# Splitting a weight tile into high and low parts in two halves instead of in one piece

## What is computed

```python
z = h @ w_in                                   # 2048 x (pool, 9 x dilated q/k/v, GLA q,k,v,r,a, 3 gates)
y = branches(z)                                # pooling, dilated attention, gated linear attention (GLA)
y = (sum of gated branches @ w_br_*) @ w_mix_out
x = x + rmsnorm(y);  x = x + rmsnorm(cross_attn(rmsnorm(x), mem_kv, w_xq, w_xo))
x = x + rmsnorm(conv_ffn(rmsnorm(x), w_up, conv_w, conv_b, w_down))
```

## Time and profile before

| | us |
|---|---|
| median of 3 runs | 2735.86 (2730.3 to 2737.19) |
| the profiled execution | 2728.69 |
| its span, first to last instruction | 2727.0 |
| mean granted clock of PE, share of full | 0.985 |
| PE busy | 2611.6 (96%) |
| DVE busy | 1549.4 (57%) |
| ACT busy | 1225.0 (45%) |
| DMA, moved | 530.80 MB, 195 GB/s |

### The profile page before, as it was taken

How to read it: one execution, slowest core, us unless ns; L and a number is a source line. 1 busy time by engine, 2 the same in 40 slices (tenths; PEclk the granted TensorE clock), 3 DMA queues, 4 the chain that set the end, 5 groups by cost and what they waited for, 6 DMA issues and landing times. The chain is left out here.

```text
span 2727.0 us, 52522 instructions
## 1 busy us (share of the span) xinstructions
PE 2611.6 (96%) x20839; PEld 2495.9 (92%) x20839; DVE 1549.4 (57%) x1940; ACT 1225.0 (45%) x1534; POOL 193.3 (7%) x303
## 2 busy tenths in 40 slices
PE   6799999999999999999999998999899999999997
PEld 5778879899999999999999988898799999999997
DVE  4455554544555555654564547454766665666666
ACT  5344444432443443443343544334555555444553
POOL 0011121100011111100000000320000000000000
PEclk9899999999999999999999999999899999999998
DMA  5686786766888888885666755865366656666563
GB/s 148 180 275 194 228 278 195 240 183 166 234 231 229 220 237 236 220 224 162 178 172 180 233 138 153 278 208 167 97 185 182 168 169 196 182 182 185 162 178 115
DMA packets 856553, 530.80 MB, mean 195 GB/s; under 512 B 13169, under 2 KB 834345, under 8 KB 855647
## 3 DMA queue, kind: packets, MB, share of 16 engines
q1 hardware_dynamic: 822583, 440.07, 58.8%
q0 software_dynamic: 25728, 83.34, 9.0%
q10 hardware_dynamic: 8128, 5.76, 0.7%
HBM read 499.79 MB, written 33.29 MB: 195 GB/s over the span
## 5 line engine op out<-in xcount | busy, mean ns | idle before, releaser
L518 DVE TENSOR_TENSOR weights_lo<-weights_raw,weights_hi 128x2048 fp32r<-128x2048 f32 x407 | 932.3, 2291 | 769.9 <-ACT weights_hi L511 769.1
L542 PE MATMUL bank<-h_hi,weights_hi 128*128 128x264 f32 x4624 | 1333.3, 288 | 35.8 <-DVE weights_lo L518 15.7
L543 PE MATMUL bank<-h_lo,weights_hi 128*128 128x264 f32 x4624 | 1314.6, 284 | 0.0
L544 PE MATMUL bank<-h_hi,weights_lo 128*128 128x264 f32 x4624 | 1313.1, 284 | 0.0
L542 PEld LDWEIGHTS bank<-h_hi,weights_hi 128*128 128x128 f32 x4624 | 875.5, 189 | 57.3 <-issue 26.2
L543 PEld LDWEIGHTS bank<-h_lo,weights_hi 128*128 128x128 f32 x4624 | 876.2, 189 | 2.0 <-issue 1.9
L511 ACT ACTIVATE weights_hi<-weights_raw 128x2048 fp32r<-128x2048 f32 x407 | 776.9, 1910 | 214.8 <-PE bank L544 205.0
L544 PEld LDWEIGHTS bank<-h_hi,weights_lo 128*128 128x128 f32 x4624 | 871.3, 188 | 0.0
L542 PE MATMUL bank<-y_hi,weights_hi 128*128 128x264 f32 x1232 | 351.9, 286 | 7.3 <-DVE y_lo L2413 3.8
L544 PE MATMUL bank<-y_hi,weights_lo 128*128 128x264 f32 x1232 | 350.6, 285 | 0.0
L543 PE MATMUL bank<-y_lo,weights_hi 128*128 128x264 f32 x1232 | 349.0, 283 | 0.0
(11 more groups left out here) (374 smaller groups left out, 2169.3 us busy)
## 6 DMA issues: line engine op xcount, KB each, us to landing
weights_raw<-in_w_in SPq DMA_DIRECT2D x177, 1024.0 KB, 6.6
weights_raw<-in_w_up SPq DMA_DIRECT2D x88, 1024.0 KB, 5.9
weights_raw<-in_w_down SPq DMA_DIRECT2D x64, 704.0 KB, 4.7
gla_state_sample<-in_state_gla POOLq DMA_DIRECT2D x32, 512.0 KB, 6.2
out_gla_s<-gla_state_sample POOLq DMA_DIRECT2D x32, 512.0 KB, 6.9
weights_raw<-in_w_br_gla SPq DMA_DIRECT2D x16, 1024.0 KB, 5.9
weights_raw<-in_w_mix_out SPq DMA_DIRECT2D x16, 1024.0 KB, 5.9
weights_raw<-in_w_xkv SPq DMA_DIRECT2D x16, 1024.0 KB, 6.0
```

Source lines behind the costliest of these rows:

```text
L518: nc.vector.tensor_tensor(w_lo[:, r, :], raw[:, r, :], w_hi[:, r, :].bitcast(F32), ALU.subtract).then_inc(lo_ready, 1)
L542: nc.tensor.matmul(out, wh, xh, start=first and n == 0, stop=False)
L543: nc.tensor.matmul(out, wh, xl, start=False, stop=False)
L544: mm = nc.tensor.matmul(out, wl, xh, start=False, stop=last and n == len(blocks) - 1)
```

## The change

Each tile is split in two halves of eight contraction blocks (1024 columns of the 2048). ACT issues two copies and counts `hi_ready` up after each; DVE waits for each half of the high part by itself, subtracts it, and counts `lo_ready` up after each. A product waits for the first half ahead of its first block and for the second half ahead of the first block that lies in it. A load waits for both halves. All counts on the two semaphores are doubled. Where two products share a tile (`fresh=False` in the second of them), only one that starts with the second half waits for it.

```diff
-        credits = [(lo_ready, RING)] + [(s, 1) for s in evac]
+        credits = [(lo_ready, 2 * RING)] + [(s, 1) for s in evac]
...
+        HALVES = [slice(0, SLOT // 2), slice(SLOT // 2, SLOT)]
...
             act.wait_ge(slot_loaded[r], (p.third(j, i) + 2) * 16)
-            nc.scalar.activation(w_hi[:, r, :], raw[:, r, :], ACT.Copy).then_inc(hi_ready, 1)
+            for half in HALVES:
+                nc.scalar.activation(w_hi[:, r, half], raw[:, r, half], ACT.Copy).then_inc(hi_ready, 1)
...
-            dve.wait_ge(hi_ready, p.c(j, i) + RING + 1)
             dve.wait_ge(projected, p.c(j, i) + 1)
-            nc.vector.tensor_tensor(w_lo[:, r, :], raw[:, r, :], w_hi[:, r, :].bitcast(F32),
-                                    ALU.subtract).then_inc(lo_ready, 1)
+            for n, half in enumerate(HALVES):
+                dve.wait_ge(hi_ready, p.c(j, i) * 2 + (2 * RING + 1 + n))
+                nc.vector.tensor_tensor(w_lo[:, r, half], raw[:, r, half], w_hi[:, r, half].bitcast(F32),
+                                        ALU.subtract).then_inc(lo_ready, 1)
...
-            sp.wait_ge(lo_ready, p.c(j, i) + 1)
+            sp.wait_ge(lo_ready, p.c(j, i) * 2 + 2)
...
             if fresh:
-                pe.wait_ge(lo_ready, p.c(j, i) + RING + 1)
+                pe.wait_ge(lo_ready, p.c(j, i) * 2 + (2 * RING + 1))
+            second = [n for n, b in enumerate(blocks) if b[0] >= SLOT // 2 and (fresh or b[0] == SLOT // 2)][:1]
...
                 wh, wl = w_hi[:, r, off:off + P], w_lo[:, r, off:off + P]
+                if n in second:
+                    pe.wait_ge(lo_ready, p.c(j, i) * 2 + (2 * RING + 2))
```

More of the change, by code:

```diff
@@ L959, in first_hi @@
                 act.wait_ge(slot_loaded[c], 16)
-                nc.scalar.activation(w_hi[:, c, :], raw[:, c, :], ACT.Copy).then_inc(hi_ready, 1)
+                for half in HALVES:
+                    nc.scalar.activation(w_hi[:, c, half], raw[:, c, half], ACT.Copy).then_inc(hi_ready, 1)
             first_hi(0)
@@ L2040, in first_lo @@
             def first_lo(c):
-                dve.wait_ge(hi_ready, c + 1)
-                nc.vector.tensor_tensor(w_lo[:, c, :], raw[:, c, :], w_hi[:, c, :].bitcast(F32),
-                                        ALU.subtract).then_inc(lo_ready, 1)
+                for n, half in enumerate(HALVES):
+                    dve.wait_ge(hi_ready, 2 * c + 1 + n)
+                    nc.vector.tensor_tensor(w_lo[:, c, half], raw[:, c, half], w_hi[:, c, half].bitcast(F32),
+                                            ALU.subtract).then_inc(lo_ready, 1)
             for t in range(KB):
```

## The result

| | before | after |
|---|---|---|
| median of the runs, us | 2735.42 (2730.3 to 2737.19, 4 runs) | 2712.48 (2711.17 to 2713.46, 4 runs) |
| the profiled execution | 2728.69 | 2713.18 |
| its span | 2727.0 | 2711.5 |
| mean granted clock of PE | 0.985 | 0.987 |

The ratio is 0.9918, with a 95% interval from 0.9906 to 0.9931: the change takes 22.9 us off the median, and 15.5 us between the two profiled executions. The prediction was 2721, from 2711 to 2733. Its sum against the profiled execution was -14.7 us, near the 15.5; against the medians it was 8 us short. The experiments deal with both.

What follows compares the result with a forecast made beforehand. PE's stream was taken as the bound, leaving only its holes to fill. Start -1.55, fifteen places -11.6 and clock -1.5 make -14.7 us, from a median of 2735.9 to 2721.2 us; range 2711 to 2733.

Steps and rivals of the forecast that it cites:

- What bounds the kernel: PE's stream, busy 2611.6 of 2727.0 us; with PE's instructions unchanged, only its holes of about 115 us can be filled.
- The cost of a half: 1024 columns cost 1.05 us on ACT and 1.22 on DVE; two halves take 1.99 and 2.36 us.
- The lockstep: Where DVE's split waits for ACT's high part, halves end the low part 0.78 us earlier, at 3.44 instead of 4.22.
- the lower bound of 0.70: Saving per lockstep split if DVE's two halves do not overlap across the new wait: 0.70 us instead of 0.78.
- Fifteen places: PE's holes waiting for small DVE results behind a lockstep split: 0.78 us each, -11.6 us in all.
- The start: Start of the GLA stage: PE begins on the first half 1.92 us earlier, setup costs +0.37, net -1.55 us.
- Waits of PE: One more wait in the middle of each product, normally long met, costs PE zero.
- something else came next: Rival: in half the places PE meets another wait, giving 2728.5 us; 18% together with a start-only case.
- DVE's idle time: Sign: DVE's idle time ahead of splits falls from 769 to about 480 us, 0.86 us off each of 340 waits.
- The clock: The 3.6 us hole ahead of 1236.4 shrinks to 2.8, so PE keeps full clock behind it: -1.5 us, between +2 and -6.
- The rival that the clock gives more: Half-clock stretch at the memory keys and part of another also go, 6 us on top: 2717 us, 15%.
- The offset: The median of the runs lies 7.2 us above the profiled run, and this was carried over to the new kernel.

Runs made afterwards that it cites:

- order: Kernel before with whole tiles, small DVE operations that PE waits for moved ahead of DVE's split; 2714.81 us, ratio 0.9922.
- places: The full change with halves kept only at 27 of 410 tiles, where a small DVE result stands behind a split, setup included; 2720.9 us, ratio 0.9956.
- elsewhere: The full change with whole tiles where small DVE results stand behind a split, halves in the other 383 tiles and the setup's three; 2728.51 us, ratio 0.9981.
- waits7: The full change with PE's second wait repeated, already met, on up to seven last blocks of each product; 2712.67 us, ratio 0.9919.
- pe_whole: The full change, but PE waits for both halves ahead of each product and has no second wait; 2714.35 us, ratio 0.9927.
- swap: The full change with DVE's two waits ahead of its first half in the order of the kernel before, high half first; 2712.88 us, ratio 0.9921.
- best: The full change plus small DVE operations moved ahead of the split, except sample states and both norms; 2698.34 us, ratio 0.9871.
- quarters: The full change with four pieces of 512 columns a tile on ACT and DVE instead of two halves; 2708.83 us, ratio 0.9911.

## Why the prediction was right, and where it was not

- **What bounds the kernel.** Right. PE's busy time did not move, and the stretch from the MLP's first product to the last norm takes 772.1 us in every trace of every kernel here.
- **The cost of a half.** Right to a hundredth: 1.052 and 1.221 us, pairs of 2.00 and 2.36.
- **The lockstep.** The mechanism is shown by order, which removes the cause and leaves the halves out. Its size per place was 0.70 to 0.73 us at ten of them and 0.87 at the memory rows, so the lower bound of 0.70 was the better value, though the overlap that it leaves out is there. One of two small terms ate the rest at each place looked at: at the dilated start DVE's first half begins 0.11 us behind the high part and not 0.03 (655.49 behind 654.33 + 1.05), and at the sample state ACT's own split comes 0.08 us later.
- **Fifteen places.** Fourteen had it. The first of the memory keys did not: 2.33 us after, as 2.2 before, because ACT was waiting for the load there, 6.7 us before and 7.6 after. The wait in the earlier trace rows names DVE, one step short of that cause, and in a third trace of before the hole is absent. The turned values gave more than their part, 0.97 each and some more: the prediction had one cause there, the split ahead, and the runs places and elsewhere show two. In sum the places and the start gave 13.2 us in the trace: 1.85 at the start, 2.1 at the sample states, 3.4 at the turned values, 0.7 at the dilated start, 1.4 at the two y_lo, 0.9 at the memory rows, 2.2 in the norms and 0.7 at the memory values. The forecast was 1.55 + 11.6 = 13.15; the agreement is partly luck, errors that cancel.
- **The start.** The +0.37 us of the setup ahead did not appear: DVE's scans, the last step that hangs on it, ended 0.07 us later than before, so most of it fell into waiting that I had not looked for. The sign that the prediction gave, a hole of 13.8 to 14.2 us, was missed at 12.07. A hole also depends on when PE comes to it, here 1.42 us later, and that is no gain.
- **Waits of PE.** Zero, as forecast, and waits7 makes it firm. Of the other rivals, something else came next at one place in fifteen, not in half, and DVE's first half did not wait for the second high part.
- **DVE's idle time** ahead of splits went from 769 to 642 us and not to 480. I took 0.86 us off all 340 waits; the mean wait fell from 2.26 to 2.02 us only. In many of them DVE had small work of its own during ACT's part. It had no effect on the time.
- **The clock.** The term was -1.5 us, from how the clock stood behind two holes in one trace, and this is the step whose ground failed. Its one place did not turn out: the hole of 3.60 us came down to 2.89, and behind it PE still ran at half clock (after, the columns of the earlier trace rows):

```profile
1226.70:1230.70 4.00, 4.00 (x20) 4.00 (x21) 0.00 (x0) 0.00 (x0) 0.00 (x0) 0.57 0.73 193
```

  Those are 20 matmuls where 19 were and 33 would have been at full clock. The half-clock stretch is 3.4 us long and not 6.8, and from the end of this hole to the next PE took 163.05 us, 0.42 less than before, where 1.7 were forecast. The copy of before shows half clock behind the very hole of 2.81 us that served as the example of no loss. Three traces of before have 82.2, 95.5 and 95.9 us at half clock. Four with the halves at all tiles and the order of before (after, pe_whole, waits7, swap) have 70.4, 73.3, 76.9 and 84.2. The runs, each of which lists its mean granted clock, say the same with more weight: 0.9825 over 39 runs of before, 0.9863 over 20 of these four kernels, where the two profiled executions differ by 0.002. Among the 39 runs of before alone, a straight line gives 1.44 us less for 0.001 more of clock (the correlation is 0.68); by that the difference is worth 5.5 us, an estimate, and if all of the lost clock had stood under PE work, 0.0038 x 2730 = 10 us. The rival that the clock gives more, at 15%, had the right direction, and even its 2717 was too high.
- **The offset.** I carried the 7.2 us between the profiled execution and the median over to the kernel after. The copies show scatter of that size (39 runs of before from 2729.36 to 2739.83), and after's profiled execution lies only 0.7 us from the median of its own runs. That is why the profiled pair fits and the medians do not; it was luck that the profiled pair came so near, and the range was only just entered, at 2712 of 2711 to 2733.
- **What stays open.** Of the 22.9 us between the medians 13.2 are shown hole by hole. The other 9.7 are not. The clock may hold 5 to 10 of them, by the two estimates above. Loads that land earlier may hold some (the run elsewhere gains 6.4 us, 2.7 to 7.7 by its interval, and some 2 of those at the turned values), though the trace of after has none of that gain. These runs do not part the two.

## What to carry to other kernels

When an engine's in-order stream holds one long operation that waits for another engine, look at what stands behind it: the price is not the long operation's own product, which a ring covers, but every small result queued behind. Cutting the operation in two took 0.7 us off each such hole, a sixth of the 4.2 us that the two engines spend on a tile; moving the small result ahead took most of the hole, where nothing it waited for was late. The halves with the moves that held were the fastest here. Before a profiled time is set against a median, take a second trace of the same kernel: what varies between the two is no part of the change.

## What the runs showed of the hardware

- Two executions of one kernel can differ in clock behind the same hole: 1.00 in one trace and 0.50 in the next behind 2.81 us, which costs some 3.3 us of time (from the first matmul of the dilated branch's outputs to the transposition of the pooling context, 170.4 and 173.7 us). Of the five traces in which this hole is 2.81 to 2.91 us long two have half clock behind it; of the nine in which it is 2.10 us or less none has.
- Executions of one kernel scatter by several us: 39 runs of before lie within 10.5 us, the 6 of waits7 within 6.8, the 5 of swap within 8.0, the 4 of best within 7.4, the 4 of after within 2.3 and the 4 of quarters within 1.6. That shorter holes make them agree better is not shown.
- The order in which two waits are written ahead of a DVE operation moves its start by 0.07 us. At the dilated start the wait for the high part is the one met last; written last, DVE starts 1.16 us behind ACT (655.49 behind 654.33), and written first 1.09 us (657.22 behind 656.13). At other tiles it is the other way round (0.03 us behind the high part in 195 of 318 tiles of after, in 131 of 320 of swap), and why is open.
- A weight tile of 1 MB, 5.8 to 7.0 us by the medians of its groups, took up to 24 us to land beside 24 cache loads of 256 KB. The stretch there took 36.9 us where ACT waited 0.2 to 1.9 us for such a load, and 46.3 where it waited 7.7.
